# A decoder trunk on one core: head of the program rewritten, first convolution tap and high halves on ScalarE

## The reference, cut

```python
for i in range(2):
    u = rmsnorm(h, norm_mix_g[i])
    m = rglru_mixer(u, ...) if i == 0 else ssd_mixer(u, ...)
    h = h + m
    h = h + swiglu(rmsnorm(h, norm_ffn_g[i]), ...)
    h = h + sigmoid(rmsnorm(h, norm_ple_g[i]) @ ple_w_gate[i]) * (p[i] @ ple_w_proj[i])
return rmsnorm(h, final_norm_g)

def rglru_mixer(u, ...):
    xr, yg = split(u @ w_in)
    xr = causal_dwconv(xr, conv_w, conv_b)     # four taps
    r, i = sigmoid(xr @ w_gate_r + ..), sigmoid(xr @ w_gate_i + ..)   # per head of 256
    ...                                        # decay a(r), scan over time
    return (hs * gelu(yg)) @ w_out
```

## Time and profile before

| | us |
|---|---|
| three runs | 2737.05, 2737.88, 2750.62 |
| median | 2737.88 |
| the profiled execution's own time | 2750.44 |
| its span, first to last instruction | 2748.7 |
| PE busy in it | 2701.8 (98%) |
| DVE, ACT, POOL busy | 2031.9, 1339.4, 364.9 |

### The profile page before, as it was taken

How to read it: one execution, slowest core, us unless ns; L and a number is a source line. 1 busy time by engine, 2 the same in 40 slices (tenths; PEclk the granted TensorE clock), 3 DMA queues, 4 the chain that set the end, 5 groups by cost and what they waited for, 6 DMA issues and landing times.

```text
span 2748.7 us, 50850 instructions
## 1 busy us (share of the span) xinstructions
PE 2701.8 (98%) x17807; PEld 2463.1 (90%) x17807; DVE 2031.9 (74%) x2818; ACT 1339.4 (49%) x1818; POOL 364.9 (13%) x410
## 2 busy tenths in 40 slices
PE   7999999999999999999999999999999999999997
PEld 7999788888888888999998999988888888888897
DVE  8888876655666677888886688888667557667776
ACT  5676344444444444446664466643444444444443
POOL 3333200000000011200001000021000000001122
PEclk9999999999999999999999999999999999999999
DMA  5555565656655555555555655545665565665654
GB/s 196 184 176 174 171 192 186 188 169 185 197 184 186 195 184 168 173 195 186 183 186 177 205 183 184 185 156 184 190 192 186 178 207 185 192 190 176 189 179 147
DMA packets 162727, 504.54 MB, mean 184 GB/s; under 512 B 18048, under 2 KB 24512, under 8 KB 161472
## 3 DMA queue, kind: packets, MB, share of 16 engines
q1 hardware_dynamic: 162544, 503.14, 57.8%
q10 hardware_dynamic: 80, 0.07, 0.0%
HBM read 500.97 MB, written 2.16 MB: 183 GB/s over the span
## 4 chain that ended last, share of the span: by engine, by line
PE 90%; DVE 8%; DMA 1%; issue 0%; ACT 0%; SPq 0%; DVEq 0%; POOL 0%; ACTq 0%
PE bank L398 39%; PE bank L400 20%; PE bank L381 10%; PE bank L383 10%; PE bank L382 10%; DVE wlo L852 3%; DVE R L885 1%; DVE h L1095 1%; DVE R L883 1%; DVE h L1094 0%; PE bank L571 0%; ACT whi L607 0%; PE bank L562 0%; DMA wraw<-in_A 0%; DVE rinvh L893 0%
## 5 line engine op out<-in xcount | busy, mean ns | idle before, releaser
L398 PE MATMUL bank<-R,whi 128*128 128x512 f32 x4992 | 1752.0, 396 | 7.9 <-DVE R L885 4.9
L852 DVE TENSOR_TENSOR wlo<-wraw,whi 128x1024 fp32r<-128x1024 f32 (+3 forms) x1056 | 1198.5, 1145 | 572.4 <-ACT whi L607 570.3
L607 ACT ACTIVATE whi<-wraw 128x1024 fp32r<-128x1024 f32 (+3 forms) x1056 | 992.9, 947 | 974.3 <-PE bank L400 744.6
L400 PE MATMUL bank<-R,wlo 128*128 128x256 f32 x4992 | 1399.9, 280 | 0.0
L398 PEld LDWEIGHTS bank<-R,whi 128*128 128x128 f32 x4992 | 937.0, 188 | 231.1 <-DVE R L885 5.5
L400 PEld LDWEIGHTS bank<-R,wlo 128*128 128x128 f32 x4992 | 943.8, 189 | 0.2
L381 PE MATMUL bank<-R,whi 128*128 128x256 f32 x2368 | 683.4, 289 | 20.9 <-DVE R L909 13.0
L383 PE MATMUL bank<-R,wlo 128*128 128x256 f32 x2368 | 672.8, 284 | 0.0
L382 PE MATMUL bank<-R,whi 128*128 128x256 f32 x2368 | 672.7, 284 | 0.0
L381 PEld LDWEIGHTS bank<-R,whi 128*128 128x128 f32 x2368 | 456.5, 193 | 30.0 <-issue 15.5
L382 PEld LDWEIGHTS bank<-R,whi 128*128 128x128 f32 x2368 | 457.3, 193 | 2.2 <-issue 1.9
(11 more groups left out here) (166 smaller groups left out, 1294.8 us busy)
## 6 DMA issues: line engine op xcount, KB each, us to landing
wraw<-in_F SPq DMA_DIRECT2D x352, 512.0 KB, 3.9
wraw<-in_B SPq DMA_DIRECT2D x224, 512.0 KB, 3.5
wraw<-in_A SPq DMA_DIRECT2D x96, 512.0 KB, 4.1
wraw<-in_F SPq DMA_DIRECT2D x128, 384.0 KB, 3.1
wraw<-in_F SPq DMA_DIRECT2D x128, 320.0 KB, 3.2
wraw<-in_PL SPq DMA_DIRECT2D x64, 320.0 KB, 3.1
wraw<-in_PL SPq DMA_DIRECT2D x64, 256.0 KB, 2.8
arena<-cs_rows SPq DMA_DIRECT2D x8, 1024.0 KB, 6.7
```

The source lines that it names most:

```text
L398: nc.tensor.matmul(dst.rearrange("p (s t) -> p s t", s=2), whi[:, q % RING, cols], src[:, :, k, :], start=first, stop=False)
L400: mm = nc.tensor.matmul(dst[:, 0:SEQ], wlo[:, q % RING, cols], src[:, 0, k, :], start=False, stop=last)
L607: nc.scalar.activation(whi[:, slot, 0:w * BLOCK], wraw[:, slot, 0:w * BLOCK], ACT.Copy).then_inc(w_hi, 1)
L852: V.tensor_tensor(wlo[:, slot, 0:w * BLOCK], wraw[:, slot, 0:w * BLOCK], whi[:, slot, 0:w * BLOCK].bitcast(F32), ALU.subtract).then_inc(w_ ...
```

## The change

Three things.
- Head of the program. PE takes the 64 blocks of the first head in eighths by `HEAD_ORDER`: k 0 to 7 of three column groups first, then the other halves; SP loads in that order, with x parts 2 and 3 behind pieces 1 and 2. PE starts with 12 matmuls of constants. ACT loads its table with a one-element Tanh before data is there, squares all 16 tiles in two instructions of 2048 columns; POOL and DVE fold one set each by three adds. The statistics follow piece 5 instead of 3, the first gates' products piece 9 instead of 7, the softplus of the decay parameters is spread, and DVE, not POOL, splits the first gates.
- In A1 the first tap with the bias (L998 of before) runs on ACT.
- In the last eight pieces of A2 and of the second B2 ACT makes the high half of the next input, for seven of eight tiles; DVE makes the low half one piece later.

```diff
@@ -45,6 +45,10 @@
+HEAD_ORDER = (0, 2, 4, 1, 3, 6, 5, 7)
+HEAD_DONE = (4, 5, 7, 8)
+WARM = 12
...
@@ -169,8 +175,10 @@
-sumsq2, square3 = ge[:, 0, :], ge[:, 1, :]
-square4 = swi4.rearrange("p (j t) -> p j t", j=4)
+sumsq2 = ge[:, 0, :]
+flat_a, flat_b = arena[:, 0:2048], arena[:, ge0:ge0 + 2048]
+square_a = flat_a.rearrange("p (j t) -> p j t", j=8)
+square_b = flat_b.rearrange("p (j t) -> p j t", j=8)
...
@@ -318,6 +326,10 @@
 p = it * n + ph["piece0"] + q
+if index == 0 and first and q < 8:
+    at0 = P * w * BLOCK * HEAD_ORDER[q]
+elif index == 0 and first and q == 8:
+    at0 = P * w * BLOCK * 8
...
@@ -329,11 +341,13 @@
 if index == 0 and first and q == 0:
-    load_x(0, 1, 2)
-if index == 0 and first and q == 1:
-    load_x(3)
+    load_x(0, 1)
+if index == 0 and first and q == 0:
+    sp.dma_start(apar[:], t["apar"]).then_inc(apar_in, 16)
+if index == 0 and first and q == 2:
+    load_x(2, 3)
 if index == 0 and first and q == 3:
-    for dst, part in ((apar, "apar"), (bpar, "bpar"), (hpar, "hpar")):
+    for dst, part in ((bpar, "bpar"), (hpar, "hpar")):
...
@@ -447,6 +461,8 @@
 pe.wait_ge(const_done, 3)
+for _ in range(WARM):
+    nc.tensor.matmul(bank[7][:, 0:P], ones[:], ones[:], start=True, stop=True)
...
@@ -494,11 +510,14 @@
 items = matmul_groups(ph, it, operand_ready)
+if norm == 0 and first:
+    pieces = [items[8 * b:8 * b + 8] for b in HEAD_ORDER]
+    items = [x for part in pieces for x in part] + items[64:]
...
     done += w
-    if norm is not None and first and q == (3 if norm == 0 else 1):
+    if norm is not None and first and q == (5 if norm == 0 else 1):
...
@@ -512,12 +531,12 @@
         decay_columns()
-if name == "A1" and q % 8 == 7:
-    head = it * 2 + q // 8
+if name == "A1" and q in ((9, 15) if first else (7, 15)):
+    head = it * 2 + q // 15 if first else it * 2 + q // 8
...
     pe.wait_ge(xc_lo, head * 2 + 2)
-    if not (first and q == 7):
+    if not (first and q == 9):
...
@@ -616,15 +635,21 @@
+act.wait_ge(const_done, 3)
+nc.scalar.activation(spare[:], ones[:, 0:1], ACT.Tanh)
+hi(0, 0, 8, early=True)
...
 for c in range(4):
-    if c < 3:
-        hi(c, c, 8, early=True)
...
                              ).then_inc(u0_hi, 1)
-nc.scalar.activation(square4, h[:, 8:12, :], ACT.Square).then_inc(square4_done, 1)
+    if c == 1:
+        hi(1, 1, 8, early=True)
+        hi(2, 2, 8, early=True)
+hi(3, 3, 8, early=True)
+nc.scalar.activation(square_a, h[:, 0:8, :], ACT.Square).then_inc(square8_done[0], 1)
+softexp(1, kt_b, kt_a)
...
@@ -708,16 +733,22 @@
 w = width_of(index, ph, q, last)
-if w:
-    hi(p + LEAD, q + LEAD, w, early=first and index == 0 and q == 0)
-if norm_of(ph) is not None and first and q == (2 if index == 0 else 1):
+if w and not (first and index == 0 and q == 0):
+    hi(p + LEAD, q + LEAD, w)
+if index == 0 and first and q == 1:
+    nc.scalar.activation(square_b, h[:, 8:16, :], ACT.Square).then_inc(square8_done[1], 1)
+if norm_of(ph) is not None and first and q == (4 if index == 0 else 1):
...
-if name == "A1" and first and q == 3:
-    softexp(1, kt_b, kt_a)
-if name == "A1" and first and q == 7:
+if name == "A1" and first and q == 9:
     act.wait_ge(kk_done, 2)
+if name in PAIRED and next_norm(ph) is not None and q > 8:
+    j = q - 9
+    k, m = next_norm(ph), it * 8 + j
+    act.wait_ge(bank_free, it * 8 + ph["group0"] + 4 + j + 1)
+    nc.scalar.activation(R[next_u(k)][:, 0, m, :], h[:, m, :], ACT.Copy,
+                         scale=gains[:, k * KT + m:k * KT + m + 1]).then_inc(uh_done, 1)
...
@@ -733,15 +764,22 @@
+taps_at = {5: 0, 6: 1} if first and q < 8 else {2: 0, 4: 1}
+if s in taps_at:
...
+    act.wait_ge(bank_free, it * 8 + ph["group0"] + 4 + hh * 4 + j + 1)
+    nc.scalar.activation(xc[:, hh, j, :], xpad[:, j, 3:3 + SEQ], ACT.Identity,
+                         bias=flat(apar[:, at(head * 2 + j), 4:5]),
+                         scale=flat(apar[:, at(head * 2 + j), 3:4])).then_inc(atap_done, 1)
 if not (first and q < 8):
-    chain_step(head - 1, 1 - hh, s)
-if s in ((4, 5) if first and q < 8 else (3, 5)):
...
+    chain_step(head - 1, 1 - hh, {0: 8, 1: 0, 2: 1}.get(s, s) if first else s)
+if s in ((6, 7) if first and q < 8 else (3, 5)):
...
     nc.scalar.activation(R[1][:, 0, 20 + j, :], xc[:, hh, j, :], ACT.Copy).then_inc(xc_hi, 1)
-if s == 4:
+if s == (2 if first and q < 8 else 4):
...
@@ -898,10 +944,9 @@
 own.mark(V.memset(xpad, 0.0))
+lo(0, 0, 8)
...
 for c in range(4):
-    if c < 3:
-        lo(c, c, 8)
...
@@ -909,36 +954,41 @@
                                ).then_inc(u_ready, 1)
+    if c == 1:
+        lo(1, 1, 8)
+        lo(2, 2, 8)
+lo(3, 3, 8)
...
+dve.wait_ge(apar_in, 16)
...
 own.close(1)
-def squares(m0):
...
+def split_first_gates():
+    dve.wait_ge(g_hi, 1)
+    V.tensor_tensor(R[1][:, 1, 16:20, :], graw[:, 0:1024].rearrange("p (k t) -> p k t", k=4),
+                    R[1][:, 0, 16:20, :].bitcast(F32), ALU.subtract).then_inc(g_lo, 1)
+def fold_squares():
+    dve.wait_ge(square8_done[1], 1)
+    own.link(V.tensor_tensor(flat_b[:, 0:1024], flat_b[:, 0:1024], flat_b[:, 1024:2048], ALU.add))
+    own.link(V.tensor_tensor(flat_b[:, 0:512], flat_b[:, 0:512], flat_b[:, 512:1024], ALU.add))
+    V.tensor_tensor(sumsq2, flat_b[:, 0:256], flat_b[:, 256:512], ALU.add).then_inc(sumsq2_done, 1)
...
-    lam = apar[:, :, 7]
-    if q == 2:
-        dve.wait_ge(params_in, 48)
...
-    elif q == 6:
+    if q == 1:
...
+    elif q == 7:
...
+        dve.wait_ge(params_in, 32)
...
@@ -1038,17 +1088,20 @@
 w = width_of(index, ph, q, last)
-if w:
+if w and not (first and index == 0 and q == 0):
...
-if norm_of(ph) is not None and first and q == (2 if index == 0 else 1):
+if norm_of(ph) is not None and first and q == (4 if index == 0 else 1):
...
 if name == "A1" and first:
-    if q < 2:
-        squares(KT - 4 + 2 * q)
-    kk_steps(q)
+    if q == 2:
+        fold_squares()
+    if q == 3:
+        split_first_gates()
+    if q < 4:
+        kk_steps(q)
...
@@ -1063,26 +1116,31 @@
 if not (first and q < 8):
-    chain_step(head - 1, 1 - hh, s)
-group = ({3: 0, 4: 1, 5: 2, 7: 3} if first and q < 8 else {1: 0, 3: 1, 5: 2, 7: 3}).get(s)
+    chain_step(head - 1, 1 - hh, {2: 8, 3: 2}.get(s, s) if first else s)
+group = ({4: 0, 5: 1, 6: 2, 7: 3} if first and q < 8 else {1: 0, 3: 1, 5: 2, 7: 3}).get(s)
...
-    dve.wait_ge(w_used, p - s + 2 * group + 2)
+    dve.wait_ge(w_used, HEAD_DONE[group] if first and q < 8 else p - s + 2 * group + 2)
...
     V.tensor_tensor(row, bank[src][:, 0:SEQ], rinv[:], ALU.mult).then_inc(bank_free, 1)
-    dve.wait_ge(bank_free, g0 + hh * 4 + j + 1)
-    conv(xpad[:, j], xc[:, hh, j, :],
...
-         tile, xc_done)
+taps_at = {5: 0, 6: 1} if first and q < 8 else {2: 0, 4: 1}
+if s in taps_at:
...
+    dve.wait_ge(atap_done, tile + 1)
+    later_taps(xpad[:, j], xc[:, hh, j, :],
...
     V.tensor_tensor(row, bank[src][:, 0:SEQ], rinv[:], ALU.mult).then_inc(bank_free, 1)
+if first and q == 7:
+    kk_steps(q)
...
@@ -1094,8 +1152,12 @@
 if next_norm(ph) is not None:
-    dve.wait_ge(bank_free, g0 + j + 1)
-    u_split(next_norm(ph), m, m + (next_norm(ph) - 1) * KT + 1, next_u(next_norm(ph)))
+    k = next_norm(ph)
+    if name in PAIRED and j > 0:
+        u_low(k, m - 1, m + (k - 1) * KT, next_u(k))
+    if name not in PAIRED or j == 7:
+        dve.wait_ge(bank_free, g0 + j + 1)
+        u_split(k, m, m + (k - 1) * KT + 1, next_u(k))
...
@@ -1278,15 +1340,10 @@
-clear(0)
-for m in range(KT // 2):
-    if m % 4 == 0:
-        pool.wait_ge(x_in[m // 4], 16)
-    add_square(0, m)
-pool.wait_ge(square4_done, 1)
-for m in range(4):
-    pool.wait_ge(sumsq_done, KT // 2 + 1 + m)
-    G.tensor_tensor(sumsq[:], sumsq[:], square4[:, m, :], ALU.add).then_inc(sumsq_done, 1)
+pool.wait_ge(square8_done[0], 1)
+own.link(G.tensor_tensor(flat_a[:, 0:1024], flat_a[:, 0:1024], flat_a[:, 1024:2048], ALU.add))
+own.link(G.tensor_tensor(flat_a[:, 0:512], flat_a[:, 0:512], flat_a[:, 512:1024], ALU.add))
+G.tensor_tensor(sumsq[:], flat_a[:, 0:256], flat_a[:, 256:512], ALU.add).then_inc(sumsq_done, 1)
...
@@ -1294,10 +1351,10 @@
 if name == "A1":
...
         for j in range(2):
-            if j == 1:
+            if j == 1 and not first:
...
```

More of the change, by code:

```diff
@@ L144, in trunk @@
         hpar = sb("hpar", [HEADS, 2])
+        spare = sb("spare", [P, 1])
         arena = sb("arena", [P, ARENA])
@@ L883, in u_split, with u_low, tile @@
                 V.tensor_scalar(tile(dst[:, 0, at(m), :]), tile(h[:, at(m), :]), g, None, ALU.mult).then_inc(uh_done, 1)
+                u_low(norm, m, count, buf)
+            def u_low(norm, m, count, buf):
+                g = gains[:, at(m + norm * KT)]
+                dst = R[buf]
+                def tile(x):
+                    return x.rearrange("p a t -> p (a t)")
                 dve.wait_ge(uh_done, count)
@@ L911, in _ @@
                                            ).then_inc(u_ready, 1)
+                if c == 1:
+                    lo(1, 1, 8)
+                    lo(2, 2, 8)
+            lo(3, 3, 8)
```

(47 more changed lines are left out.)

14 lines of the change are left out of this document (8 added, 6 removed).

## The result

| | before | after |
|---|---|---|
| median, us | 2737.88 (7 executions) | 2722.78 (7 executions) |
| lowest and highest | 2736.55 to 2750.62 | 2721.29 to 2724.61 |
| profiled execution, its span | 2750.44, 2748.7 | 2724.61, 2722.8 |

The ratio is 0.992 with an interval of 0.989 to 0.995: faster by 0.8%. The prediction said 2715.1 (2708 to 2730); the time lies inside the range, 7.7 us above the forecast. Before, one execution takes 2737 and the next 2750 (four and three of the seven here); after, all lie within 3.3 us. So the median of before is one of its better executions, and its medians in the later sets of runs are 2745 to 2751.

The account below looks back on a forecast made before the run. PE was taken as the bound, busy 2701.8 of 2748.7 us, so only its waits, clock and matmul speed count. 10.6 (head) plus 12.2 (A2, second B2) gave 22.8 off the median 2737.9: 2715.1 us, range 2708 to 2730.

Parts of the forecast that it names:

- Part 2: Ends of A2 and second B2: DVE's period falls from 3.64 to 3.2, PE's waits and low clock go, 12.2 us.
- The port rule: A2 and second B2: two-SBUF-input DVE and SBUF-reading POOL instructions exclude each other, single-input ones do not; period 3.2 or 3.97.
- Part 1: Head of the program: new order starts the first matmul near 8.2 and piece 10 at 48.2 instead of 58.84, 10.6 us.
- The slow pace in one or both layers: Wide matmuls at the slower pace: one layer 2727.7 us, chance 0.20; both layers 2740.3, chance 0.03.
- The head does not do what it says: Head: DVE's chain stays as long, early start is given back at the gates; Part 1 gives 5, 2720.7 us; chance 0.06.
- a DVE period that stays as it was: A2 and second B2: POOL takes L883's place, period stays 3.6, Part 2 gives -1.2, 2728.5 us; chance 0.14.

Follow-up runs that it names:

- late last tile: Version with tap and gates on DVE, plus two dead DVE multiplications ahead of tile 15 in A2 and the second B2; executions from 2716.70 to 2734.76 us.
- the old head alone: Kernel before, with only the high halves moved to ACT in A2 and the second B2; head and A1 unchanged: 2723.87 us.
- everything but the high halves: Changed kernel, but DVE again makes both halves in A2 and the second B2: 2751.51 us, ratio 1.000.

## Why the prediction was right, and where it was off

- **Part 2 (12.2 us) held.** Alone it gave 11 within its own set (14.0 against the 2737.88). The waits for L852 and L885 went, and the 1.7 us of low clock twice. DVE's period was sized 3.2 and is 2.82 in A2 and 2.77 in the second B2, PE's own time for eight blocks at its two paces; what POOL holds up shows in L890, 1.64 for 1.22, about 0.4 and not 0.6 to 0.7. Tile 15 has 2.3 us to spare, not none.
- **The port rule** that spoke against this edit (the Trainium skill, SBUF — State Buffer, Who interferes with whom) agrees with the traces in both places, and still left the gain. In A1 a POOL instruction of 2.94 stretched a DVE tap of 0.48 to 2.63, and that is a link of the ring. In A2 POOL's square (308.31 to 308.92) comes just ahead of L890 (308.36), which takes 0.42 more; then POOL's add waits for L890 and takes 1.60 instead of the 0.80 of the earlier trace rows, the end of it under the bank reads. POOL got in once per period, and it was POOL that paid for the second time. What the prediction says of an instruction with a single SBUF input is too wide: the page says it only outside of DVE's 2-port modes (no trace shows in which mode an instruction ran), and L921, which has one such input, took 0.71 beside POOL's square (325.32, above) and 0.34 without POOL beside it (late last tile, 321.2).
- **Part 1, up to piece 10**: first matmul 8.23 (predicted 8.2), gates 43.4 (45.4), piece 10 at 46.4 (48.2). L896 was not held up (L901 took 1.26); `lo` of piece 4 was (2.38). PE waited 1.3 there (before piece 4), not 2.1.
- **The step that failed** is the last of Part 1: "Removed with no gain: DVE's 0.4 us for L998, 16 times; in A1 PE does not wait for it. ACT has room for it." ACT's room is an average (50% busy). The tap stands on a chain through ACT, DVE and POOL that before ended 0.95 us ahead of the gates, and it makes that chain 27.2 us long where PE needs 25.92. The tap, with the later place of the other taps, costs 5.0 to 6.5 us. It was priced at nothing.
- **The same step also carried the gain wrongly.** Piece 10's start was counted as if the rest of A1 would shift with it. A start earlier by 12.5 us only lasts if the chain behind it is shorter than PE's time. With the tap back on DVE, gates of head 1 come 10.2 us earlier than with the old head alone (65.09, 75.33), of the last head 7.7 (223.40, 231.06), and the time is 7.6 lower. With the gate weights on DVE too the last gates come 11.0 earlier (220.08), and the time is 11.6 lower (other set; the profiled spans, 2722.1 and 2710.3, differ by 11.8): there the predicted 10.6 arrive.
- **The rivals.** The slow pace in one or both layers did not occur in any of 47 executions of the nine kernels that have no wait for tile 15; with the wait both layers can run slow: 7 of the 53 executions of before on record lie two steps up, which the four that the prediction had did not show. "The head does not do what it says" gave 2720.7 and comes nearest; its mechanism was named as DVE's chain in the head, while the loss lies behind the head. By the last gates, 229.71 in after, 223.40 with the taps back and 220.08 with both edits, the tap takes 6.3 us and the gate weights on POOL 3.3: 2715.1 + 9.6 = 2724.7, and the 1.9 us down to the measured 2722.8 are not assigned.
- **Luck.** The range reached to 2730 for the slow pace and for a DVE period that stays as it was. Neither came; the loss that did come, 9.6 us in A1, was in no term and happened to fit in. And the sum starts from a median that stood among before's better executions in the prediction's three runs and again, four to three, in the result. Of all 53 executions of before, 20 lie at 2733 to 2741, 26 at 2748 to 2754 and 7 at 2763 to 2769.

Open: why the pace has two values, and what decides between them. The wait for tile 15 is not the only place where it changes. In eight of the nine profiles with no such wait A2 ended at 353.3 ns per block, and the pace went to 346.7 where F1 begins, at the two matmuls of the sum of squares and without a wait (after: 353.3 up to 329, 346.7 from 331 on). In the profile of before the second layer's pace went from 346.7 to 353.3 at 1853.87, behind a wait of 0.58 us for L852 (one of 0.59 us just before it left it as it was), and back at the wait for tile 15. In everything but the high halves it went up at 1844.7, where one block took 400 ns, and stayed through all the waits behind. So each change looked at here stands at an interruption of the row of blocks, and what is shown is only this: with the wait for tile 15 the rest of the layer ran at either pace, without it always at the better one.
